# Fetching the rows of peer_v for two expert blocks in one transfer

## The reference

```
q = (xn @ w_q)                                # 8 heads, two halves of 128
scores = q . sub_keys; top 16 of each half; top 16 of their 256 sums
idx, gate                                     # 8*16 = 128 of 16384 experts per token
ub = take(u_tab, idx); vb = take(v_tab, idx)  # rows of 1024 floats
hid = gelu(einsum('td,ted->te', xb, ub))
y   = einsum('te,ted->td', hid * gate, vb)
```

## Time and profile before

| | |
|---|---|
| median of 3 runs | 2696.3 us (2694.12 to 2697.71) |
| the profiled execution | 2700.7 us, of which 2698.6 us are the span of the core |
| PE busy | 2453.7 us, 91% of the span |
| DVE busy | 1720.4 us, 64% |
| ACT busy | 885.1 us, 33% |
| POOL busy | 519.7 us, 19% |
| mean granted clock of PE | 0.925 |
| moved by DMA | 433.62 MB, 161 GB/s on average |
| issues of v | 128 of 512 KB, median 5.8 us to landing |
| issues of u | 128 of 512 KB, median 5.6 us to landing |
| issues of the gates | 32 of 768 KB, median 7.5 us to landing |

### The profile page before, as it was taken

How to read it: one execution, slowest core, us unless ns; L and a number is a source line. 1 busy time by engine, 2 the same in 40 slices (tenths; PEclk the granted TensorE clock), 3 DMA queues, 4 the chain that set the end, 5 groups by cost and what they waited for, 6 DMA issues and landing times.

```text
span 2698.6 us, 33009 instructions
## 1 busy us (share of the span) xinstructions
PE 2453.7 (91%) x12813; PEld 2069.1 (77%) x12813; DVE 1720.4 (64%) x3229; ACT 885.1 (33%) x1500; POOL 519.7 (19%) x521
## 2 busy tenths in 40 slices
PE   8787997877878899869899999889999999999998
PEld 7676776877877788748666578678888888888997
DVE  3378884433524374342597889668888888887665
ACT  1232786020120343222333244323333333333332
POOL 0597500010000000000000000133333333333210
PEclk7787997867868899989999999989999999999999
DMA  5442310000000222312333346889998889898762
GB/s 220 133 137 90 110 48 1 1 1 1 0 0 31 78 94 94 110 62 79 105 105 108 111 154 215 289 298 321 313 324 311 322 314 324 312 355 304 250 211 94
DMA packets 212191, 433.62 MB, mean 161 GB/s; under 512 B 21736, under 2 KB 127889, under 8 KB 211793
## 3 DMA queue, kind: packets, MB, share of 16 engines
q1 hardware_dynamic: 167104, 268.35, 29.5%
q0 software_dynamic: 44800, 161.24, 16.9%
q10 hardware_dynamic: 144, 2.10, 0.2%
HBM read 389.96 MB, written 41.68 MB: 160 GB/s over the span
## 4 chain that ended last, share of the span: by engine, by line
PE 49%; ACT 1%; DVE 1%; issue 1%; DMA 0%; POOL 0%; ACTq 0%; DVEq 0%; POOLq 0%
PE bank L1721 20%; PE bank L1612 10%; PE bank L1707 4%; PE bank L1705 4%; PE bank L1706 4%; PE bank L1676 3%; PE bank L1694 2%; PE bank L1598 1%; ACT ha L1757 1%; PE bank L1628 1%; DMA ug<-in_peer_u_dram,gidx 0%; DVE o_nat L1998 0%; DVE o_nat L1997 0%; ACT scores L1764 0%; DVE ug L1944 0%
## 5 line engine op out<-in xcount | busy, mean ns | idle before, releaser
L1612 PE MATMUL bank<-h2f,ua_T 128*128 128x384 f32 x832 | 297.7, 490 | 9.1 <-ACT ha L1757 9.1
L1721 PE MATMUL bank<-vt_hi,wg_hi 128*128 128x512 f32 x768 | 248.0, 404 | 3.8 <-DVE wg_lo L1988 3.6
L1721 PE MATMUL bank<-vt_lo,wg_hi 128*128 128x512 f32 x768 | 238.5, 392 | 0.0
L1721 PE MATMUL bank<-vt_hi,wg_lo 128*128 128x512 f32 x768 | 238.3, 391 | 0.0
L1705 PE MATMUL bank<-h_hi,uT_hi 128*128 128x384 f32 x608 | 211.1, 347 | 0.0
L1612 PEld LDWEIGHTS bank<-h2f,ua_T 128*128 128x128 f32 x832 | 145.5, 190 | 84.4 <-issue 16.7
L1567 POOL DMA_INDIRECT ug<-in_peer_u_dram,gidx x128 | 141.9, 1109 | 344.0 <-DVE ug L1944 340.7
L1970 DVE TENSOR_TENSOR vt_lo<-vt_raw,vt_hi 128x1024 fp32r<-128x1024 f32 x128 | 156.5, 1223 | 80.7 <-ACT vt_hi L1840 80.7
L1707 PE MATMUL bank<-h_hi,uT_lo 128*128 128x384 f32 x608 | 204.9, 337 | 0.0
L1706 PE MATMUL bank<-h_lo,uT_hi 128*128 128x384 f32 x608 | 204.2, 336 | 0.0
L1572 POOL DMA_DIRECT2D hid_keep<-ha x52 | 28.3, 544 | 899.2 <-ACT ha L1757 899.2
(11 more groups left out here) (389 smaller groups left out, 5504.2 us busy)
## 6 DMA issues: line engine op xcount, KB each, us to landing
u_raw<-in_peer_u_dram SPq DMA_DIRECT2D x128, 512.0 KB, 5.6
vt_raw<-in_peer_v_dram SPq DMA_DIRECT2D x128, 512.0 KB, 5.8
gates<-g_stage SPq DMA_DIRECT2D x12, 2048.0 KB, 8.3
gate<-gates SPq DMA_DIRECT2D x32, 768.0 KB, 7.5
pj_raw<-in_w_in_dram SPq DMA_DIRECT2D x16, 1024.0 KB, 5.4
ada_w<-in_w_ada_dram POOLq DMA_DIRECT2D x32, 512.0 KB, 4.6
mx_raw<-in_w_in_dram SPq DMA_DIRECT2D x12, 1024.0 KB, 5.2
hid_keep<-ha POOLq DMA_DIRECT2D x52, 192.0 KB, 2.1
```

What stands on the lines that cost most here:

```text
L1612: last = pe.matmul(bank[6][:, 0:TD], uT[b % 2][:, k, :], m.h2f[:, k, P:], start=(k == 0), stop=(k == KC - 1))
L1721: ins = pe.matmul(y_bank[t][q][:], w[n % 2][:, tok], v[n % 2][:, 512 * q:512 * q + 512], start=(first and i == 0), stop=(last and i == 2))
```

## The change

Two buffers of 8 KB per partition (v_pair, in the places of the four) take the rows of two blocks each. SP fetches block 2r and 2r+1 in one transfer of 1 MB, at even steps only; it waits until DVE has written v_lo of block 2r-3, the last one that read the buffer. The rows of the two blocks lie side by side in the table, so each partition takes 8 KB in one piece of DRAM. ACT and DVE read half a buffer each time. What is computed, and how often, is the same, and the other transfers and their waits keep their places in the loop.

```
-    v_raw = [m.at(f"vt_raw{i}", [P, D], off) for i, off in enumerate((132, 136, 104, 108))]
+    v_pair = [m.at(f"vt_raw{i}", [P, 2, D], off) for i, off in enumerate((132, 104))]
...
-    s_v = [m.sem(f"ex_v{i}") for i in range(4)]
+    s_v = [m.sem(f"ex_v{i}") for i in range(2)]
...
-            def load_v(n):
-                if n >= 4:
-                    sp.wait_ge(x["vlo"], n - 3)
-                sp.dma_start(v_raw[n % 4][:], v_dram[:, n, :]).then_inc(s_v[n % 4], 16)
+            def load_v(r):
+                if r >= 2:
+                    sp.wait_ge(x["vlo"], 2 * r - 2)
+                sp.dma_start(v_pair[r % 2][:], v_dram[:, 2 * r:2 * r + 2, :]).then_inc(s_v[r % 2], 16)
...
-                    for n in range(4):
-                        load_v(n)
+                    for r in range(2):
+                        load_v(r)
...
-                if n >= 4:
-                    load_v(n)
+                if n >= 4 and n % 2 == 0:
+                    load_v(n // 2)
...
-                act.wait_ge(s_v[n % 4], 16 * (n // 4 + 1))
+                act.wait_ge(s_v[n // 2 % 2], 16 * (n // 4 + 1))
...
-                nc.scalar.activation(v_hi[n % 2][:], v_raw[n % 4][:], ACT.Copy).then_inc(x["vhi"], 1)
+                nc.scalar.activation(v_hi[n % 2][:], v_pair[n // 2 % 2][:, n % 2, :], ACT.Copy).then_inc(x["vhi"], 1)
...
-                v.tensor_tensor(v_lo[n % 2][:], v_raw[n % 4][:], v_hi[n % 2][:].bitcast(F32), ALU.subtract)\
+                v.tensor_tensor(v_lo[n % 2][:], v_pair[n // 2 % 2][:, n % 2, :], v_hi[n % 2][:].bitcast(F32), ALU.subtract)\
                     .then_inc(x["vlo"], 1)
```

## The result

The changed kernel takes 2699.56 us (median of 20 runs, 2694.08 to 2708.89), the kernel before 2694.82 us (median of 20, 2690.28 to 2703.59). The ratio is 1.0020, with a 95% interval of 1.0010 to 1.0029, which is 2.7 to 7.8 us; the medians differ by 4.7 us. The forecast was slower by 12.3 us, within 2694 to 2733; the direction held, the size was 2.6 times too large.

What follows compares the result with a forecast made beforehand. TensorE was taken to bound the kernel, with DMA close behind. Late u in gate rounds (9.3 us) plus the x2 round (3 us) made 12.3 us on the median of 2696.3, forecasting 2708.5 us, range 2694 to 2733.

Steps and rivals of the forecast that it cites:

- What bounds the kernel: Whole last loop: TensorE sets the end, DMA close behind; only a transfer too late for TensorE changes the time.
- The pair came in time: Merged v transfer: expected to land after 7.7 us, read after 16.2 us, so worth 0.
- The bytes saved and the issues saved: SP's queue: same bytes, 64 issues of 0.33 us fewer, in a queue that waits 570.6 us; worth 0.
- a sum of 0 + 3 us: Alternative total if some 2 us fixed cost per transfer were paid in the queue, making u 1 us later.
- u in the gate rounds: Every second even expert, 25 rounds: u lands later, some exceed the 12.58 us lead; TensorE loses 9.3 us.
- the 3.0 us: How much later u was taken to land in each gate round, between bounds of 0 and 4.5 us.
- the gap behind v: While v of the odd expert arrives, engines move 230 GB/s against 395 later; 0.42 MB was to be had there.
- The 1.6 us behind v's issue: Start of the v transfer, first part of its 4.4 us, which nothing was supposed to fill.
- the row at 0.16 MB/us: Pace of gate and u beside the gathers, 1.31 MB in 8.19 us; 0.72 MB at it gives 4.5 us.
- rival 1: Gate rounds: the gap takes the extra bytes, u up to 2.4 us later; 0 to +5 us overall, chance 0.35.
- u in the round with x2: Near 2413 us, u of 98 lands behind the pair and four x2n transfers; 1 to 7 us, taken as 3.
- The other rounds, head and tail: Rounds without gates, first four rows of v, and experts from 104 on: enough lead or DMA room, 0.

Runs made afterwards that it cites:

- e2: Kernel before with its four single 512 KB buffers, but v of both blocks issued at the moment of the pair: 2699.46 us, ratio 1.0011.
- e5: Kernel before, but in gate rounds v of the even expert, and hl behind it, issued only once u has landed: 2694.54 us, ratio 1.0003.
- e3: Changed kernel with one more 512 KB transfer ahead of the gates in 21 gate rounds: 2709.36 us, ratio 1.0055.
- e4: Kernel before with one more 512 KB transfer ahead of the gates in the same 21 rounds: 2697.05 us, ratio 1.0004.
- e7: Changed kernel with two more 512 KB transfers ahead of the gates in 21 rounds: 2735.44 us, ratio 1.0151.
- e8: Kernel before with two more 512 KB transfers ahead of the gates in 21 rounds: 2696.16 us, ratio 1.0001.
- e1: Changed kernel with the four x2n transfers issued at block 112 in place of 96: 2695.04 us, ratio 1.0001.
- e9: Changed kernel with x2n issued at block 98, right behind u of that block in place of ahead of it: 2696.42 us, ratio 1.0009.

## Why the prediction was right in direction and wrong in size

*What bounds the kernel: right.* TensorE sets the end, no wait for v appeared, and all that the change could do was to make a transfer late. The pair came in time: by its packets it landed in the gate rounds after 5.9 us on average where 7.7 was expected, and L1841 has no wait for DMA.

*The bytes saved and the issues saved: right, worth 0.* The 64 issues fewer changed neither DMA's rate (319 and 317 GB/s) nor the time. The Trainium skill, "DMA: Bandwidth & Descriptors", asks in its section "Rules for kernel authors" for at least 1 MiB in one DMA, and its section on the anatomy of one DMA has a fixed cost of some 2 us. Paid on each transfer in the queue, that cost would have led to a sum of 0 + 3 us. That is nearer to the measured time, but not for its reason: e2, with transfers of 512 KB at the same moments, lands u only 0.6 us later, so nothing like 2 us is paid for each in this queue.

*u in the gate rounds: the step that failed.* This term was mis-sized: it said that u lands 3.0 us later in each gate round and that TensorE loses 9.3 us in all, and the runs show 0.2 us later and no stop, 0 us. The mechanism was right: only what is ahead of u counts (e5), the change put 0.72 MB ahead of it, and that room is gone (e3 against e4, e7 against e8). The lead of 12.58 us, 25 rounds and the landings were read rightly. Both parts of the 3.0 us were too dear. I let the gap behind v take 0.42 MB and priced the other 0.30 at 3.0 us, 10 us/MB. A dose on top of a filled gap cost 4.6 us/MB (e3), a second one 3.6 (e7). At 4.6 the 0.8 us of e2 are 0.17 MB paid, so the gap took some 0.55, and the 0.2 us of the changed kernel leave it nearly all of the 0.72; these two are estimates from that price. The 1.6 us behind v's issue that I took as closed to further bytes were too long: in the kernel before, v's first packet moves 0.96 us behind the issue at 2035.83. The 3.0 was taken nearer to the row at 0.16 MB/us; that is the rate at which gate and u moved beside the gathers, and it isn't what a further byte costs. The engines' whole rate was 395 GB/s, 2.5 us/MB, and the measured price lies between the two. Either correction takes the term to next to nothing: with the gap at 0.42 MB and the price at 4.6, for one, u is 1.4 us later, the slowest row of 11.1 us becomes 12.5, and the term is 0. That is rival 1 (0.35).

*u in the round with x2: right.* Predicted 1 to 7 us, taken as 3; the stop is 4.1 us. The queue did run dry ahead of the pair, as the upper part of that range supposed: from 1.3 us before the pair's issue at 2393.09 to 0.9 us behind it, SP's queue moves a single packet.

```profile
DMA packets 160, 0.59 MB, mean 266 GB/s; under 512 B 17, under 2 KB 17, under 8 KB 160
## 3 DMA queue, kind: packets, MB, share of 16 engines
q0 software_dynamic: 159, 0.59, 86.7%
q1 hardware_dynamic: 1, 0.00, 0.0%
```

(2391.8 to 2394.0, in the changed kernel.) What was left out is the lower clock behind the stop, 1.5 us, although a fall of the clock after stops was named as what would make the prediction wrong. This term is the whole loss that the runs can find.

*The other rounds, head and tail: right, 0.* Sum by the runs: 0 + 4.1 + 1.5 = 5.6 us, measured 4.7 (2.7 to 7.8). Stop and clock are those of one execution; e2's, with a stop of 3.3 us, kept its clock.

That the direction held rests on the smaller term alone: without the x2 round the same reasoning, rightly sized, gives no change, and e1 measures none.

## What to carry to other kernels

Merging two transfers into one moves one of them in time, and the question is which urgent transfer now stands behind it: look for the load with the smallest lead over its use, in the rarest round, since an average round (here 12.58 us of lead, 9.8 to landing) can be harmless where the one with a bulk transfer in front is not. Price further bytes in a shared queue with a dose on the chip, not with the average rate of that queue in its busiest stretch. And a bulk load with a late deadline belongs behind the urgent one of its step, or into a stage where DMA has room.

## What was not expected of the hardware

SP's issue instructions themselves can take longer: the four of x2n took 2.23 us before and 3.51 after, and the dose in e3 up to 2.38 us where its median is 0.43. This delays what is issued behind them, though u of 98 would have stood behind x2n's bytes all the same. The cause isn't shown: in e9 the same four took 2.33 us with u in the queue ahead of them as well. And a stop does not always bring TensorE's clock down: all those of up to 1.8 us in e3, the one of 3.3 in e2 and most in e7 left it full, while the one of 4.1 us cost 1.5 us more at half of it.
